# Two steps' scores in one product, a shorter router chain, and weight sums handed to GpSimd in a two-layer decoder trunk

## The reference, cut to what matters

```python
for layer in range(2):
    h = rms_norm(x, norm1[layer]); proj = h @ w_in[layer]
    # 8 query heads, 2 KV heads, three branches (compressed, selected, window), 4 blocks of 128 queries
    s = einsum('btgrd,bsgd->bgrts', q, k) * scale + head_bias(dist); p = masked_softmax(s, mask)
    o = gc[..., 0:1] * o_cmp + gc[..., 1:2] * o_slc + gc[..., 2:3] * o_win
    x = x + concatenate([rms_norm(o), rms_norm(conv)]) @ w_out[layer]
    h = rms_norm(x, norm2[layer])
    if layer == 0: x = x + (silu(h @ wg) * (h @ wu)) @ wd
    else:
        logits = h @ router_w + router_b
        top_logit, top_idx = top_k(logits, 2); weights = softmax(top_logit)
        # rows of each expert: y = (silu(xs @ wg[e]) * (xs @ wu[e])) @ wd[e]; x[token] += weight * y
```

## Time and profile before

| what | value |
|---|---|
| median of 3 runs | 2070.72 us (2070.32 to 2074.26) |
| profiled execution, its own time | 2073.83 us |
| its span, first to last instruction | 2072.1 us |
| PE busy | 2041.4 us, 99% |
| PEld busy | 1485.8 us, 72% |
| DVE, ACT, POOL busy | 680.9, 313.0, 95.4 us |
| mean granted TensorE clock | 0.997 |

### The profile page before, as it was taken

One profiled execution on the slowest core, in us unless ns is written; L12 is line 12 of the kernel. 1 busy time (PEld: TensorE's weight loads), 2 busy tenths in 40 slices (PEclk: granted clock), 3 DMA queues, 4 the chain that ended last, 5 costly groups with the idle time before them and its releaser, 6 DMA issues.

```text
span 2072.1 us, 29315 instructions
## 1 busy us (share of the span) xinstructions
PE 2041.4 (99%) x12170; PEld 1485.8 (72%) x12170; DVE 680.9 (33%) x1430; ACT 313.0 (15%) x823; POOL 95.4 (5%) x103
## 2 busy tenths in 40 slices
PE   8999999999999999999999999999999999999998
PEld 4545547888864444555499999999999996565654
DVE  2256644333234313666420000000000015555353
ACT  2234411111100013433100000000000001111110
POOL 2100010000000011000020000000000000000110
PEclk9999999999999999999999999999999999999999
DMA  8211112222240152100188567778777777888991
GB/s 331 80 41 42 41 48 92 82 82 82 97 167 0 64 213 82 41 1 1 42 335 337 218 243 277 263 284 296 280 290 281 285 279 287 312 328 310 328 364 71
DMA packets 51461, 377.94 MB, mean 182 GB/s; under 512 B 6875, under 2 KB 7051, under 8 KB 24066
## 3 DMA queue, kind: packets, MB, share of 16 engines
q1 hardware_dynamic: 43984, 355.75, 45.8%
q0 software_dynamic: 5904, 15.93, 2.7%
q10 hardware_dynamic: 1442, 4.39, 0.6%
HBM read 367.41 MB, written 10.90 MB: 183 GB/s over the span
## 4 chain that ended last, share of the span: by engine, by line
PE 96%; DVE 2%; issue 1%; ACT 1%; POOL 0%; DMA 0%; DVEq 0%; ACTq 0%; POOLq 0%
PE ps L602 22%; PE ps L1661 13%; PE ps L620 11%; PE ps L685 9%; PE ps L1471 7%; PE ps L1677 6%; PE ps L1408 5%; PE ps L670 5%; PE ps L1592 5%; PE ps L1536 2%; PE ps L1523 2%; PE ps L1548 2%; PE ps L1414 1%; PE ps L1377 1%; PE ps L554 0%
## 5 line engine op out<-in xcount | busy, mean ns | idle before, releaser
L602 PE MATMUL ps<-work,arena 128*128 128x136 f32 (+3 forms) x3712 | 477.5, 287 | 0.6 <-DVE work L893 0.6
L602 PEld LDWEIGHTS ps<-work,arena 128*128 128x128 f32 x3712 | 465.0, 190 | 2.8 <-issue 1.6
L620 PE MATMUL ps<-hid,arena 128*128 128x136 f32 (+2 forms) x1760 | 236.0, 287 | 0.0
L899 DVE TENSOR_TENSOR hid<-sg,ps 128x136 f32<-128x136 f32 (+3 forms) x116 | 35.4, 305 | 601.3 <-ACT sg L1140 600.9
L620 PEld LDWEIGHTS ps<-hid,arena 128*128 128x128 f32 x1760 | 225.2, 190 | 0.4 <-issue 0.4
L1471 PE MATMUL ps<-hT,arena 128*128 128x512 f32 x384 | 185.4, 596 | 0.0
L685 PE MATMUL ps<-arena,work 128*64 128x256 f32 x1320 | 163.2, 381 | 2.4 <-DVE hid L899 1.4
L1661 PE MATMUL ps<-hT,arena 128*128 128x256 f32 x704 | 155.7, 379 | 0.0
L1661 PEld LDWEIGHTS ps<-hT,arena 128*128 128x128 f32 x704 | 133.7, 190 | 18.6 <-issue 0.5
L685 PEld LDWEIGHTS ps<-arena,work 128*64 128x64 f32 x1320 | 100.1, 137 | 55.0 <-issue 11.2
L1140 ACT ACTIVATE sg<-ps 128x136 f32<-128x136 f32 (+3 forms) x116 | 33.8, 292 | 611.1 <-PE ps L602 604.1
(11 more groups left out here) (331 smaller groups left out, 1791.0 us busy)
## 6 DMA issues: line engine op xcount, KB each, us to landing
arena<-m_w SPq DMA_DIRECT2D x110, 1536.0 KB, 6.8
arena<-m_w SPq DMA_DIRECT2D x66, 1024.0 KB, 10.9
arena<-m_w SPq DMA_DIRECT2D x66, 512.0 KB, 5.1
arena<-f_gu SPq DMA_DIRECT2D x11, 2048.0 KB, 8.0
arena<-w_cv SPq DMA_DIRECT2D x8, 1536.0 KB, 23.7
arena<-w_o SPq DMA_DIRECT2D x4, 2048.0 KB, 8.5
arena<-f_dn SPq DMA_DIRECT2D x4, 2048.0 KB, 7.7
arena<-w_q SPq DMA_DIRECT2D x4, 1024.0 KB, 8.8
```

Source lines behind the costliest of these rows:

```text
L602: m = mm(ps[:, bank_of(i, s), j * CAP:j * CAP + W], w[:, k, :], xT[:, k, 0:W], start=(k == 0), stop=(k == KD - 1))
L620: m = mm(ps[:, 2 + j // 2, (j % 2) * CAP:(j % 2) * CAP + W], down_w[s % NSLOT][:, j * P:(j + 1) * P], hid[:, s % 2, 0:W], start=(s == 0 an ...
```

## The change

1. *Scores.* For `t < JOINT = 2` the two branches' scores of a head come from one product of `2 n` columns in the even step, and the odd step issues none. VectorE reads the odd step's scores from column `n` on.
2. *Router.* The last tile's scaling (`norm_tile`) is split: its power is started (`last_tile_power`), and the scaling into `hn` (`last_tile_scaled`) comes behind the mask. The first expert is found by the maximum of `key` instead of by the rank; the ranks' comparison and reduction come behind the first `pick`.
3. *Weight sums.* Order of the sums: 1, 1, 2, 2, 3, 3, 4, 4, the first half of sum 3 moved from the end of the pair before into the pair. Sums 1 for the next pair come right behind L969 in all pairs; in a round's first pair sum 2 comes behind L991. In round 7 `hidden` of tile 0 precedes sum 2.
4. *GpSimd.* In rounds 5 and 6 sum 4 is made by GpSimd (`fourth_sums`), counted in `b_sums`, for all five pairs behind the gather of the next expert's rows. Product 4 waits for it there, and VectorE's next `weight_sum2` waits for the first half, which reads what it overwrites.

```diff
-        COPY2, WSUM1, WSUM2, WSUM3, WSUM4 = 1, (1, 2), (3, 5), (4, 6), (7, 8)
+        COPY2, WSUM1, WSUM2, WSUM3, WSUM4 = 1, (1, 2), (3, 4), (5, 6), (7, 8)
...
+        fourth_at = lambda q, k: HSUM4 + 2 * q + k
...
-                pe.wait_ge(w_sums, r * (8 * NQ) + sum_at(q, WSUM4[1]))
+                if lead(i):
+                    pe.wait_ge(w_sums, r * (8 * NQ) + sum_at(q, WSUM4[1]))
+                else:
+                    pe.wait_ge(b_sums, fourth_at(q, 2))
                 product(4, 0, a22, b21, False)
...
+                if len(tiles) == 1:
+                    dve.wait_ge(power_out, powers[0])
...
             v.tensor_tensor(msk, oh[:, 0], oh[:, 1], ALU.add).then_inc(mask_done, 1)
+            last_tile_scaled()
...
-            after(v.tensor_tensor(sq1, bc_mid(key, 1, E), bc_last(key, E), ALU.is_gt))
-            after(v.tensor_reduce(rank, sq1, AX, ALU.add))
-            after(v.tensor_scalar(first_e, rank, 0.0, None, ALU.is_equal))
+            after(v.tensor_reduce(total, key, AX, ALU.max))
+            after(v.tensor_scalar(first_e, key, total, None, ALU.is_equal))
...
                 if t == 0:
+                    after(v.tensor_tensor(sq1, bc_mid(key, 1, E), bc_last(key, E), ALU.is_gt))
+                    after(v.tensor_reduce(rank, sq1, AX, ALU.add))
...
             def weight_sum2(r, q, e):
                 b11, b12, b21, b22 = quarters(q)
+                if e == 0 and 0 < q <= 2 * NQ:
+                    dve.wait_ge(b_sums, fourth_at(q - 1, 1))
...
                 weight_sum2(r, q, 1)
+                weight_sum3(r, q, 0)
                 weight_sum3(r, q, 1)
-                weight_sum4(r, q, 0)
-                weight_sum4(r, q, 1)
+                if lead(i):
+                    weight_sum4(r, q, 0)
+                    weight_sum4(r, q, 1)
...
-                if u == 0 and not lead(i):
-                    dve.wait_ge(q_ps[5], product_at(q))
-                    weight_sum1(r, q + 1, 0)
-                    weight_sum1(r, q + 1, 1)
...
+                if u + 1 < NQ:
+                    weight_sum1(r, q + 1, 0)
+                    weight_sum1(r, q + 1, 1)
...
-                if u == 0 and not lead(i):
+                if 0 < u < NQ - 1:
                     weight_sum2(r, q + 1, 0)
-                elif u + 1 < NQ:
-                    weight_sum1(r, q + 1, 0)
-                    weight_sum1(r, q + 1, 1)
-                    weight_sum2(r, q + 1, 0)
-                    weight_sum3(r, q + 1, 0)
                 dve.wait_ge(act1_done, r * NQ + hidden_at(q))
                 v.tensor_tensor(hid_n[:, 3 * P:4 * P], hid_n[:, 3 * P:4 * P], ps[:, 0, P:2 * P], ALU.mult).then_inc(hid1_done, 1)
-                if u == 0 and not lead(i):
-                    weight_sum3(r, q + 1, 0)
+                if u == 0:
+                    weight_sum2(r, q + 1, 0)
...
                 weight_sum1(r, q, 1)
+                hidden(r, LAST, 0, P)
                 weight_sum2(r, q, 0)
-                hidden(r, LAST, 0, P)
-                weight_sum3(r, q, 0)
...
+            def fourth_sums(i, u):
+                q = pairs(i) + u
+                b11, b12, b21, b22 = quarters_of(4 * u)
+                pool.wait_ge(q_ps[2], product_at(q))
+                for e in range(2):
+                    pool.wait_ge(w_sums, sum_at(q, WSUM2[e]))
+                    nc.gpsimd.tensor_tensor(b21[e], b21[e], b11[1] if e else wt2_first, ALU.subtract).then_inc(b_sums, 1)
...
                 gather(i)
+                if i - 1 in SPLIT:
+                    for u in range(NQ):
+                        fourth_sums(i - 1, u)
...
+                    if t < JOINT and b:
+                        return
...
+                    if t < JOINT:
+                        for g in range(G):
+                            mm(ps[:, g, 0:2 * n].rearrange("p (b n) -> p b n", b=2), qT[g * DH:(g + 1) * DH, r, t * P:(t + 1) * P],
+                               kT[g * DH:(g + 1) * DH, :, 0:n], start=True, stop=True).then_inc(s_ps, 2)
+                        return
...
-                    norm_tile(2 * L + 1, TT - 1)
+                    last_tile_power()
```

More of the change, by code:

```diff
@@ L54 @@
 OUT_BANK = ((3, 1), (0, 2))
+JOINT = 2
 STEP_FILL = ((1, 1, 1), (1, 1, 1), (1, 1, 0)) + 9 * ((1, 1, 0), (2, 1, 0), (2, 1, 0))
@@ L416, in build @@
         c_at = lambda q, k: SPLIT_C + 3 * q + k
-        sum_at = lambda q, k: SPLIT_SUMS + 8 * q + k
+        sum_at = lambda q, k: SPLIT_SUMS + 6 * min(q, 2 * NQ) + 8 * max(q - 2 * NQ, 0) + k
+        fourth_at = lambda q, k: HSUM4 + 2 * q + k
         hidden_at = lambda q: NPAIR + q + 1
@@ L787, in moe_products, with moe_vector @@
                 last_round(r)
-        def moe_vector(dve, after):
+        def moe_vector(dve, after, powers, last_tile_scaled):
             for tiles in (range(TT - 1), (TT - 1,)):
                 dve.wait_ge(rl_ps, 1 if len(tiles) > 1 else 2)
+                if len(tiles) == 1:
+                    dve.wait_ge(power_out, powers[0])
                 for t in tiles:
@@ L1004, in split_round @@
                     weight_sum2(0, q, 0)
-                    weight_sum3(0, q, 0)
                 hidden(0, i, FT - 1, P)
@@ L1056, in round @@
                         weight_sum2(0, 0, 0)
-                        weight_sum3(0, 0, 0)
                 if i == SPLIT[0] - 1:
@@ L1774, in rsqrt, with rsqrt_sum @@
                 dve.wait_ge(power_out, powers[0])
-            def rsqrt_sum(dst, src, part, n):
+            def rsqrt_sum(dst, src, part, n, wait=True):
                 powers[0] += 1
                 v.scalar_tensor_tensor(dst, src, 1.0 / n, part, ALU.mult, ALU.add).then_inc(power_in, 1)
-                dve.wait_ge(power_out, powers[0])
+                if wait:
+                    dve.wait_ge(power_out, powers[0])
             v.memset(exponent, -0.5)
@@ L1807, in norm, with last_tile_power, last_tile_scaled @@
                 norm_copy(ns, TT - 1)
+            def last_tile_power():
+                dve.wait_ge(left_done, 2 * TT)
+                after(v.tensor_scalar(ss_part[:, TT - 1:TT], ss_left[:, TT - 1:TT], 1.0 / D, EPS, ALU.mult, ALU.add))
+                dve.wait_ge(ss_done, 4 * TT)
+                rsqrt_sum(rstd[:, TT - 1:TT], ss[:, TT - 1:TT], ss_part[:, TT - 1:TT], D, wait=False)
+            def last_tile_scaled():
+                v.scalar_tensor_tensor(hn[:, TT - 1, :], x[:, TT - 1, :], rstd[:, TT - 1:TT], gb[:, :], ALU.mult, ALU.mult).then_inc(xn_done, 1)
             def norm_tile(ns, t):
@@ L1960, in scores @@
                     n = P * (t + 1)
-                    dve.wait_ge(s_ps, NU * L + u + 1)
+                    joint = t < JOINT
+                    at = n * (p % 2) if joint else 0
+                    dve.wait_ge(s_ps, NU * L + (u // 4 * 4 + (2 if u % 4 == 0 else 4) if joint else u + 1))
                     if u >= 2:
                         dve.wait_ge(p_done, NU * L + u - 1)
-                    v.tensor_tensor_reduce(sb_s[:, u % 2, 0:n], ps[:, u % 2, 0:n], T[:, h, 384 - P * t:384 - P * t + n],
+                    v.tensor_tensor_reduce(sb_s[:, u % 2, 0:n], ps[:, u % 2, at:at + n], T[:, h, 384 - P * t:384 - P * t + n],
                                            -1.0, 3e38, ALU.add, ALU.min, negm[:, u % 16:u % 16 + 1]).then_inc(sb_done, 1)
@@ L2182, in _ @@
             layer(1)
-            moe_vector(dve, after)
+            moe_vector(dve, after, powers, last_tile_scaled)
         @block.scalar
```

## The result

The changed kernel takes 2076.76 us (median of 8 runs, 2075.55 to 2079.95); the kernel before 2070.83 us (8 runs beside it). The ratio is 1.0028, 95% interval 1.0019 to 1.0037: slower by 5.9 us, where 7 us of gain were forecast.

The account below looks back on a forecast made before the run. TensorE, busy 99% of the span, was taken as the bound. Gains of 2.3 (scores), 2.9 (router) and 2.3 (last round) less 0.45 made 7.05 us: 2070.72 to 2063.7 us, range 2060.5 to 2073.

Parts of the forecast that it names:

- So this part is 0: Rounds five and six: moving the fourth sums to GpSimd neither gains nor loses time, 0 us.
- the room of product four: Rounds five and six: product four can wait for GpSimd's second subtraction, 7.4 us in the first pair, over 13 later.
- The rival with the exclusion: Rounds five and six: GpSimd's second subtraction delays VectorE's second third sum and product seven; 7.25 us at T = 2.4; chance 0.20 + 0.10.
- T: Length in us of one GpSimd subtraction in rounds five and six, expected up to 2.4.
- no row shows the two engines in each other's way: Rounds five and six: argument against GpSimd holding up VectorE's third sum, taken from the profile of the kernel before.
- that the first starts only behind the gather does not matter: Rounds five and six: GpSimd's first subtraction, starting after the 0.9 us gather, makes nothing late.
- Scores in two steps: Attention: joint score products for two steps save 1.15 us a layer, 2.3 us in all; bounds 0.8 and 3.4.
- the other odd steps, too, lose 0.1 to 0.15: Attention: basis of the lower bound 0.8 us, odd steps losing that many us each to copies they no longer cover.
- Router: Router chain: earlier mask removes TensorE's 1.8 us wait and the low clock after it; 2.9 us gained, bounds 1.85 and 2.9.
- Last round: Last round: reordered sums remove two TensorE waits, on `hid` and L991; 2.3 us gained, lower bound 2.0.
- The second term: Last round, first pair's end: the 1.0 us wait on L991 and 0.2 us restart go, 1.19 us.
- Round five's first pair: Two sums now stand between L969 and L991, so the next pair's product one starts late: 0.45 us lost, once.

Follow-up runs that it names:

- fourth sums on VectorE: The whole change, but the fourth weight sums of rounds five and six stay on VectorE: 2066.77 us, ratio 0.9981 to the kernel before.
- GpSimd later: The whole change, but GpSimd starts a pair's two subtractions only when VectorE has finished both third sums: 2067.29 us, ratio 0.9984 to the kernel before.
- old order: The kernel before with GpSimd's fourth sums alone, one third sum of each pair still made in the pair before: 2072.01 us, ratio 1.0004.
- half width: The whole change, but GpSimd subtracts only 512 of the 1024 elements of each fourth sum: 2067.01 us, ratio 0.9980 to the kernel before.
- the one with one input: The whole change, but VectorE's third sums in rounds five and six are one-input negations in place: 2070.02 us, ratio 0.9992 to the kernel before.
- its own run: The kernel before with only the router part of the change: 2068.51 us, ratio 0.9986.
- both with the scores merged and the copy first: ScalarE's copy before the second exponential, fourth sums on VectorE: whole change with first pairs' next sums put back, 2062.18 us; rounds five and six as before, 2060.59.

## Why the prediction was wrong, point by point

**Rounds five and six: this step failed.** "So this part is 0" rested on TensorE's and VectorE's shares and on the room of product four. Both were read rightly: VectorE's work was hidden, product four was never late, GpSimd's subtraction lay inside the bounds (2.36 us, at their upper end). But the step took GpSimd's instruction as one that runs *beside* VectorE's. The rival with the exclusion had the mechanism right: at T = 2.36 it gives 0.66 us for each later pair and 6.9 in all; measured were 0.70 in six of these pairs and 7.2 in all. It had 0.66 for the two second pairs too, which lost 1.02, and 1.3 and 0.3 for the two first ones, which lost 1.02 and nothing, so part of the agreement of the totals is luck. Its chance was set by the trace of before, where "no row shows the two engines in each other's way". In that trace GpSimd is idle in these rounds; it could show nothing, and the missing row was counted as evidence. All experiments on it (fourth sums on VectorE, GpSimd later, old order, half width) fit the exclusion, and the one with one input showed that it is wider than two-input instructions. Even with the exclusion the rival's total (2070.9) is 5.9 us under the result: product six (2.6 us) and the attention (2.2 us) are most of that.

**What the rival left out.** Product six, 2.6 us. The first subtraction was said to be harmless ("that the first starts only behind the gather does not matter"), since only its user, product four, was looked at, not the sum of VectorE that runs at the same time. In both rounds' second pairs it starts late because of an order the change itself makes.

**Scores in two steps.** Net 2.3 us forecast, 0.13 measured, and that is under the bound of 0.8. The step that failed is "the other odd steps, too, lose 0.1 to 0.15" at worst: at t = 1 they lose 0.21, 0.31 and 0.46 us to ScalarE's copy. The rest of the step-by-step sum stood: with the copy in time each of the first three pairs at t = 1 gives its 0.21 us, and the merging 2.24 us in all. It could be read in the trace of before, where L2307 ran from 141.94 to 142.18 in such a step and the next score product started at 142.12: without that product `values` would have been due before its copy was there.

**Router.** 2.9 us forecast, 2.8 measured (1.89 + 0.50 + 0.42), 2.7 by its own run. The steps hold: no wait on the mask; the pick (L831) starts at 1034.62 and L556 follows it at 1034.99; the filling products end before it; no low clock there.

**Last round.** 2.3 forecast, 2.68 between the two traces, 1.49 and 1.20 for its two waits. The second term is the predicted 1.19. Of the first, 1.14 was predicted: the wait of the earlier trace rows was 1.4 us in that execution and 1.1 in two others of kernels with the same last round, so 2.3 is the usual worth.

**Round five's first pair.** 0.45 us forecast, 0.42 measured. In round six's first pair I expected L991 to be in time by 0.4 us; it cost 0.36 in the second.

The sum as it came out: -0.1 (scores), -2.8 (router), -2.7 (last round), +0.8 (hidden product), +9.8 (GpSimd) = +5.0 us. The medians have 5.9.

## What to carry to other kernels

- Handing hidden work from VectorE to GpSimd is no relief where both work on SBUF: ask which VectorE instruction stands in the queue at the moment GpSimd is released, and who waits for it. A release between two queued instructions was the worst place here (7.2 us); behind the last of them it cost 0.4 us, where a later VectorE instruction ran into it.
- An engine that is idle in a stretch of the trace says nothing on what happens when it isn't. A rival of that kind deserves the weight of its mechanism, not of the missing row.
- When a product is taken out, look at what its time covered on the other engines, and at the order *within* those engines: the missing 2.2 us lay behind one exponential.

## What the runs showed of the hardware

- GpSimd's subtraction of 128x1024 takes 2.36 us (VectorE's 1.22), 128x512 takes 1.27.
- While one of the two works on such a subtraction in SBUF, the other's stands still: VectorE's then took up to 3.39 us, GpSimd's 3.28.
- VectorE's one-input multiplication, SBUF to SBUF, 128x1024 in 0.68 us, is held off by GpSimd too, up to 2.86 us. An addition of 128x256 with one input in PSUM is not: all 20 that ran while GpSimd worked took 0.42 to 0.43 us, as elsewhere (the run with GpSimd later).
- The granted clock of 0.50 (1.2 for 2.4 GHz) did not follow each standstill. The kernel before had it behind both waits, of 2.3 us behind layer 0 and of 1.8 us at the router. The kernel before with GpSimd's part has the same two waits. Windows (length, five engines, granted clock), behind the first wait in the kernel before, and behind both in the kernel with GpSimd's part, which shows full clock:

```profile
277.20:280.80 3.60, 3.36 (x4) 1.51 (x5) 2.07 (x6) 1.45 (x4) 1.27 (x3) 0.53 0.91 340
```
```profile
276.80:280.40 3.60, 3.32 (x8) 1.63 (x9) 2.07 (x6) 1.45 (x4) 1.31 (x3) 1.00 0.89 347
1036.50:1040.00 3.50, 3.01 (x15) 1.94 (x14) 3.13 (x17) 0.00 (x0) 0.00 (x0) 1.00 0.01 2
```

  Where the clock stayed up, the stretch behind the first wait was 1.6 to 1.7 us shorter (this kernel and both with the scores merged and the copy first), the one behind the second 0.9 (this kernel). Five executions of the kernel before that ran beside the others have a mean clock of 0.999 where most have 0.997 or 0.998; they took 2070.75 to 2071.24 us, no less than the rest. So it isn't shown that the 0.9 us of the router's gain that came from the clock are there against every execution of the kernel before. What decides stays open.
